# Two of each stage's weight rests computed by GpSimd instead of VectorE, in a fused 12-stage fp32 block kernel

## What is computed

```python
def swiglu(x, w13, w2):
    a, b = jnp.split(x @ w13, 2, axis=-1)
    return (jax.nn.silu(a) * b) @ w2
for l in range(DEPTH):        # first block
    x = layer_norm(ALPHA * x + 0.5 * swiglu(x, ffn1_w13[l], ffn1_w2[l]), ln_g[l, 0], ln_b[l, 0])
    m = mixer(x, w_in[l], ...)
    x = layer_norm(ALPHA * x + m, ln_g[l, 1], ln_b[l, 1])
    x = layer_norm(ALPHA * x + 0.5 * swiglu(x, ffn2_w13[l], ffn2_w2[l]), ln_g[l, 2], ln_b[l, 2])
for layer in range(DEPTH):    # second block
    h = swiglu_2(rms_norm(x, g[0]), ffn_w_in[layer, 0], ffn_w_out[layer, 0])
    x = x + 0.5 * rms_norm(h, g[1])
    h = token_mixer(rms_norm(x, g[2]), mix_w_in[layer], ...)
    x = x + rms_norm(h, g[3])
    h = swiglu_2(rms_norm(x, g[4]), ffn_w_in[layer, 1], ffn_w_out[layer, 1])
    x = x + 0.5 * rms_norm(h, g[5])
```

## Time and profile before

| what | value |
|---|---|
| median of 3 runs | 2111.23 us |
| the profiled execution, its own time | 2110.42 us |
| its span, first to last instruction | 2108.7 us |
| TensorE busy (matmuls) | 2092.6 us, 99% |
| VectorE busy | 1685.4 us, 80% |
| ScalarE busy | 1082.3 us, 51% |
| GpSimd busy | 80.7 us, 4% |
| granted TensorE clock | 1.000 |

### The profile page before, as it was taken

The page is one execution under the profiler, slowest core; times in us unless marked ns, Lnnn a source line. Parts: engine busy times, 40 slices in busy tenths (PEclk is TensorE's granted clock), DMA queues, the critical chain, the costliest instruction groups (busy, mean ns, idle before and its releaser), DMA issues.

```text
span 2108.7 us, 28912 instructions
## 1 busy us (share of the span) xinstructions
PE 2092.6 (99%) x10580; PEld 1776.2 (84%) x10580; DVE 1685.4 (80%) x3158; ACT 1082.3 (51%) x1568; POOL 80.7 (4%) x128
## 2 busy tenths in 40 slices
PE   9999999999999999999999999999999999999998
PEld 7888999888888899988878887988887888888887
DVE  6888766888888867778888887779888888678886
ACT  5445554544544455444454446575445445766443
POOL 0000010000000000000000001010000000101000
PEclk9999999999999999999999999999999999999999
DMA  7765755666566584557656766346665765645663
GB/s 249 235 194 175 221 168 156 188 218 191 177 218 193 176 234 143 187 168 224 196 153 213 215 190 196 126 135 208 212 197 166 225 192 168 185 140 161 211 191 106
DMA packets 314368, 395.56 MB, mean 188 GB/s; under 512 B 17972, under 2 KB 272212, under 8 KB 313972
## 3 DMA queue, kind: packets, MB, share of 16 engines
q1 hardware_dynamic: 309120, 375.52, 58.0%
q0 software_dynamic: 4944, 18.14, 2.7%
q10 hardware_dynamic: 164, 0.06, 0.0%
HBM read 392.59 MB, written 1.06 MB: 187 GB/s over the span
## 4 chain that ended last, share of the span: by engine, by line
PE 94%; DVE 3%; ACT 1%; issue 1%; DMA 0%; POOL 0%; DVEq 0%; POOLq 0%; SPq 0%; ACTq 0%
PE bank L310 26%; PE bank L312 26%; PE bank L311 26%; PE bank L304 4%; PE bank L305 4%; PE bank L306 4%; DVE w_lo L294 1%; PE bank L491 1%; PE bank L1472 1%; PE bank L1493 1%; PE bank L1002 1%; PE bank L1564 1%; ACT w_hi L287 0%; DVE xh L831 0%; DVE x L806 0%
## 5 line engine op out<-in xcount | busy, mean ns | idle before, releaser
L287 ACT ACTIVATE w_hi<-stage 128x1024 fp32r<-128x1024 f32 x711 | 746.8, 1058 | 635.4 <-PE bank L312 537.5
L294 DVE TENSOR_TENSOR w_lo<-stage,w_hi 128x1024 fp32r<-128x1024 f32 x711 | 864.8, 1224 | 213.6 <-ACT w_hi L287 206.6
L310 PE MATMUL bank<-w_hi,xt_hi 128*128 128x512 f32 x1760 | 692.0, 393 | 6.5 <-DVE xt_lo L846 5.6
L312 PE MATMUL bank<-w_hi,xt_lo 128*128 128x512 f32 x1760 | 685.5, 389 | 0.0
L311 PE MATMUL bank<-w_lo,xt_hi 128*128 128x512 f32 x1760 | 685.3, 389 | 0.0
L477 DVE STREAM_TRANSPOSE hidden<-hidden 32x128 f32<-32x128 f32 (+1 forms) x1376 | 391.7, 285 | 21.3
L310 PEld LDWEIGHTS bank<-w_hi,xt_hi 128*128 128x128 f32 x1760 | 330.5, 188 | 77.2 <-DVE xt_lo L846 4.6
L312 PEld LDWEIGHTS bank<-w_hi,xt_lo 128*128 128x128 f32 x1760 | 330.4, 188 | 69.1
L311 PEld LDWEIGHTS bank<-w_lo,xt_hi 128*128 128x128 f32 x1760 | 330.6, 188 | 66.4
L310 PE MATMUL bank<-w_hi,mt_hi 128*128 128x512 f32 x768 | 303.3, 395 | 0.2 <-DVE mt_lo L561 0.2
L312 PE MATMUL bank<-w_hi,mt_lo 128*128 128x512 f32 x768 | 299.4, 390 | 0.0
(11 more groups left out here) (279 smaller groups left out, 1387.5 us busy)
## 6 DMA issues: line engine op xcount, KB each, us to landing
stage<-in_ffn_w SPq DMA_DIRECT2D x352, 256.0 KB, 3.2
stage<-in_ffn_w_in SPq DMA_DIRECT2D x352, 256.0 KB, 3.2
stage<-in_ffn_w SPq DMA_DIRECT2D x88, 512.0 KB, 3.7
stage<-in_ffn_w_out SPq DMA_DIRECT2D x88, 512.0 KB, 3.7
stage<-in_w_in SPq DMA_DIRECT2D x80, 512.0 KB, 3.9
stage<-in_mix_w_in SPq DMA_DIRECT2D x56, 512.0 KB, 4.2
stage<-in_w_out SPq DMA_DIRECT2D x16, 512.0 KB, 4.2
stage<-in_mix_w_out SPq DMA_DIRECT2D x16, 512.0 KB, 3.5
```

The source lines that it names most:

```text
L287: act.activation(w_hi[:, u % RING, :], stage[:, u % STAGED, :], ACT.Copy).then_inc(S["hi_ready"], 1)
L294: dve.tensor_tensor(w_lo[:, u % RING, :], stage[:, u % STAGED, :], f32(w_hi[:, u % RING, :]), ALU.subtract).then_inc(S["lo_ready"], 1)
L310: pe.matmul(o, m_hi, hi, start=first, stop=False)
L312: return pe.matmul(o, m_lo, hi, start=False, stop=last)
```

## The change

GpSimd takes the rests of units +4 and +5 of every stage but the first (22 units, `BY_POOL`). It does both in one go, after the power for tile 0 of the stage before and in front of everything else it has for that transition. They have a semaphore of their own, `lo_by_pool`, and whoever waited for `lo_ready` (TensorE in `unit`, SyncE in `load`) waits through `rest_taken` for the one that counts this unit. VectorE's calls of `lo_upto` end one unit earlier where the fifth and sixth unit were due. To make room for a semaphore, the small table steps that counted `lb_step` now count on in `tables_out`; those instructions are the same.

```diff
+BY_POOL = [f + k for f in FIRST[1:-1] for k in (4, 5)]
...
+        def rest_taken(eng, u):
+
+            if u in BY_POOL:
+                eng.wait_ge(S["lo_by_pool"], BY_POOL.index(u) + 1)
+            else:
+                eng.wait_ge(S["lo_ready"], u + 1 - sum(p < u for p in BY_POOL))
+
         def load(sp, u, *halves):
 
             if u >= STAGED:
-                sp.wait_ge(S["lo_ready"], u - STAGED + 1)
+                rest_taken(sp, u - STAGED)
...
             for u in range(lo_next[0], min(end, FIRST[-1])):
-                dve.wait_ge(S["hi_ready"], u + 1)
-                dve.tensor_tensor(w_lo[:, u % RING, :], stage[:, u % STAGED, :], f32(w_hi[:, u % RING, :]),
-                                  ALU.subtract).then_inc(S["lo_ready"], 1)
+                if u not in BY_POOL:
+                    dve.wait_ge(S["hi_ready"], u + 1)
+                    dve.tensor_tensor(w_lo[:, u % RING, :], stage[:, u % STAGED, :], f32(w_hi[:, u % RING, :]),
+                                      ALU.subtract).then_inc(S["lo_ready"], 1)
                 lo_next[0] = u + 1
 
+        def pool_rests(pool, s):
+
+            for u in (FIRST[s] + 4, FIRST[s] + 5):
+                pool.wait_ge(S["hi_ready"], u + 1)
+                pool.tensor_tensor(w_lo[:, u % RING, :], stage[:, u % STAGED, :], f32(w_hi[:, u % RING, :]),
+                                   ALU.subtract).then_inc(S["lo_by_pool"], 1)
+
         def unit(pe, u):
-            pe.wait_ge(S["lo_ready"], u + 1)
+            rest_taken(pe, u)
...
                 dve_norm_start(dve, s - 1, 1)
-                if STAGES[s - 1] == "mix2":
-                    dve_norm_var(dve, s - 1, 1)
+                if STAGES[s - 1] != "mix2":
+                    lo_upto(dve, b + (5 if STAGES[s - 1] == "ffn" else 6))
+                dve_norm_var(dve, s - 1, 1)
                 lo_upto(dve, b + 6)
-                if STAGES[s - 1] != "mix2":
-                    dve_norm_var(dve, s - 1, 1)
                 dve_norm_x(dve, s - 1, 1)
...
-                lo_upto(dve, b + n + 5)
+                lo_upto(dve, b + n + 4)
                 dve_xt(dve, s + 1, 0)
...
                 for t in range(NT):
                     pool_norm(pool, s, t)
+                    if t == 0 and s + 1 < len(STAGES):
+                        pool_rests(pool, s + 1)
                     if BLOCK2 <= s + 1 < len(STAGES):
                         pool_pre(pool, s + 1, t)
```

More of the change, by code:

```diff
@@ L112, in build @@
         S = {n: ctx.enter_context(nc.semaphore(n)) for n in PER}
-        for n in ("hi_ready", "lo_ready", "used", "x_in0", "x_in1", "x_rest", "first_half", "const_in", "rest_in", "ones_set", "tables_in",
-                  "tables_turned", "tables_out", "lb_step", "x_out", "held", "rows_in",
+        for n in ("hi_ready", "lo_ready", "lo_by_pool", "used", "x_in0", "x_in1", "x_rest", "first_half", "const_in", "rest_in", "ones_set", "tables_in",
+                  "tables_turned", "tables_out", "x_out", "held", "rows_in",
                   "gu_done0", "silu0", "silu1", "gated0", "gated1", "h_turned", "h_blocks",
@@ L875, in act_lower_bounds @@
         def act_lower_bounds(act):
-            act.wait_ge(S["lb_step"], 3)
-            act.activation(lb_tmp[:, 3:5, :], lb_tmp[:, 1:3, :], ACT.Exp).then_inc(S["lb_step"], 1)
+            act.wait_ge(S["tables_out"], 6)
+            act.activation(lb_tmp[:, 3:5, :], lb_tmp[:, 1:3, :], ACT.Exp).then_inc(S["tables_out"], 1)
         def dve_tables(dve):
@@ L887, in dve_tables @@
             mx = lb_tmp[:, 0, :]
-            dve.tensor_tensor(mx, lbr_tab[:, 0, :], lbr_tab[:, 1, :], ALU.max).then_inc(S["lb_step"], 1)
-            dve.wait_ge(S["lb_step"], 1)
+            dve.tensor_tensor(mx, lbr_tab[:, 0, :], lbr_tab[:, 1, :], ALU.max).then_inc(S["tables_out"], 1)
+            dve.wait_ge(S["tables_out"], 4)
             for l in range(2):
-                dve.tensor_tensor(lb_tmp[:, 1 + l, :], lbr_tab[:, l, :], mx, ALU.subtract).then_inc(S["lb_step"], 1)
+                dve.tensor_tensor(lb_tmp[:, 1 + l, :], lbr_tab[:, l, :], mx, ALU.subtract).then_inc(S["tables_out"], 1)
         def dve_lower_bounds(dve):
             mx, e = lb_tmp[:, 0, :], lb_tmp[:, 3:5, :]
[L895 to L904, removed]
+            dve.wait_ge(S["tables_out"], 7)
+            dve.tensor_tensor(lb_tmp[:, 5, :], e[:, 0, :], e[:, 1, :], ALU.add).then_inc(S["tables_out"], 1)
+            dve.wait_ge(S["tables_out"], 8)
+            dve.reciprocal(mx, lb_tmp[:, 5, :]).then_inc(S["tables_out"], 1)
+            dve.wait_ge(S["tables_out"], 9)
+            dve.tensor_tensor(lb_tab[:, 1, :], e[:, 1, :], mx, ALU.mult).then_inc(S["tables_out"], 1)
+            dve.memset(lb_tab[:, 0, :], 0.0).then_inc(S["tables_out"], 1)
+            dve.wait_ge(S["tables_out"], 11)
+            dve.tensor_scalar(om_tab, lb_tab, -1.0, 1.0, ALU.mult, ALU.add).then_inc(S["tables_out"], 1)
+            dve.wait_ge(S["tables_out"], 12)
         def w_cols(w, c0, n, k0=0, nk=KD):
@@ L1166, in dve_mix1 @@
             dve_norm_start(dve, s - 1, 1)
+            lo_upto(dve, base + 5)
+            dve_norm_var(dve, s - 1, 1)
             lo_upto(dve, base + 6)
-            dve_norm_var(dve, s - 1, 1)
             dve_norm_x(dve, s - 1, 1)
```

## The result

| kernel | median | lowest to highest | runs |
|---|---|---|---|
| before | 2111.15 us | 2110.16 to 2111.27 | 4 |
| with the change | 2138.07 us | 2137.54 to 2138.86 | 4 |

The ratio is 1.0127, 95% interval [1.0115, 1.0139]: slower by 26.9 us. The sign was forecast, and 2138 lies in the range (2112 to 2141), but the forecast of 2128 took in only 16.7 of the 26.9 us, and 2138 is above the 2120 to 2137 that the prediction gave its own mechanism.

What follows compares the result with a forecast made beforehand. TensorE (PE) bounds the kernel, busy 2092.6 of 2108.7 us; a possible 6.9 us gain is lost to holds. Losses 2.3 + 10.2 + 4.2 = 16.7 us on 2110.4, with the median 0.8 higher, give 2128 us; range 2112 to 2141.

Steps and rivals of the forecast that it cites:

- Whether it runs beside VectorE: GpSimd's reads and VectorE instructions with two SBUF inputs exclude each other; waiting GpSimd goes first; PSUM readers are free.
- How long a rest takes: GpSimd's subtraction of 1024 columns, estimated from its selections: 2.0 us, lower end 1.04, upper end 3.1.
- D: Duration of one rest on GpSimd, taken as 2.0 us.
- R: Time in which a rest on GpSimd reads, taken as 1.9 us.
- Into stages 1, 3, 4: GpSimd's first rest goes before VectorE's of +3; `xt_lo` later by R - 1.13 = 0.8 us each, 2.3 in all.
- Into stages 6, 7, 9, 10: Both GpSimd rests hold VectorE; `xt_lo` later by 2R - 1.13 = 2.7 us each, 10.2 in all, less stage 6's 0.5.
- Into stages 8 and 11: Tile 1's power queues behind GpSimd's rest of +5; x late by D + 0.1 = 2.1 us each, 4.2 in all.
- Into stages 2 and 5, and SyncE's queue: The hold on VectorE is covered by its wait for `xt_hi`; loads queued behind rests have cover enough: 0 us.
- One hold instead of two: Rival: GpSimd's second rest waits out VectorE's rest of +3; stages 6, 7, 9, 10 lose 0.8 us each; 2120, chance 0.11.
- Hardly held: Rival: VectorE runs between pieces of GpSimd's reads; 6.9 us gain less 4.2 of stages 8 and 11; 2108.5, chance 0.10.
- faster: Rival: VectorE hardly held and both tensors read at once, D = 1.04; 4.6 us won, 2106.6, chance 0.10.
- Far slower: Rival: GpSimd's rest takes 3 us and more, or VectorE's PSUM reads are held too; 2141 and above, chance 0.09.

Runs made afterwards that it cites:

- early_fourth: Against the kernel before: GpSimd takes only unit +4's rest in stages 1, 3, 4, 6, 7, 9, 10, without waiting for VectorE's rest of +3; 2122.89 us.
- halves_6_7_9_10: Against the kernel before: GpSimd takes the two rests of stages 6, 7, 9, 10 only, each as two instructions of 512 columns; 2115.83 us.
- norm_first_8_11: Against the kernel before: GpSimd's rests in stages 8 and 11 only, +4 after tile 0's power and +5 after tile 1's; 2113.84 us.
- only_1_3_4: Against the kernel before: GpSimd takes the two rests of stages 1, 3 and 4 alone; 2114.51 us, ratio 1.0015.
- only_2_5: Against the kernel before: GpSimd takes the two rests of stages 2 and 5 alone; 2112.43 us, ratio 1.0006.
- late_fourth: Against the kernel before: GpSimd takes only +4's rest in stages 1, 3, 4, 6, 7, 9, 10, after VectorE's rest of +3; 2106.09 us.
- warm: The changed kernel with 12 transposes of a constant before the wait for x into stages 6, 7, 9, 10, 8 and 11; 2136.72 us.
- only_8_11: Against the kernel before: GpSimd takes the two rests of stages 8 and 11 alone; 2119.50 us, ratio 1.0037.

## Why the prediction was right, and where it was short

- **PE bounds, and only its waits at the transitions count.** The place was right: every loss stands at the eleven transitions. That PE's waits are all of it was not, as below.
- **Whether it runs beside VectorE (it does not).** Right, by two rows of short instructions: the earlier trace rows showed in small what `early_fourth`, `halves_6_7_9_10` and `norm_first_8_11` show in full. The Trainium skill (SBUF - State Buffer, Who interferes with whom) says that a VectorE instruction with at most one SBUF input, outside the modes with two ports, does not contend with GpSimd; the trace agrees: all 48 of `xt_lo` after the change take 0.67 to 0.69 us, and the 10 into stages 1 to 5 lie under a rest of GpSimd.
- **How long a rest takes.** D was 2.40 us for 2.0, R 2.2 for 1.9. The pace of the selections over one tensor was the wrong row to lean on for an operation over two. The figure of the Trainium skill (GPSIMD Engine Reference, 3.1 Elementwise; 2.25 us as an estimate from it) was nearer, and still 6% low. In the sum this is 3 x 0.3 for stages 1, 3, 4, up to 4 x 0.6 for 6, 7, 9, 10 and 2 x 0.4 for 8 and 11: with D and R as measured the prediction's own formulas give 3 x 1.1 + (4 x 3.3 - 0.5) + 2 x 2.5 = 21.0, which is 2132.
- **Into stages 1, 3, 4.** 2.3 forecast, 3.5 measured as gaps (3.1 by `only_1_3_4`); the formula with R = 2.2 gives 3.2, so it was the size of R.
- **Into stages 6, 7, 9, 10.** The mechanism was right, both holds are in the timeline, and 10.2 stand against 10.9 us of gaps. But the term is short by the 7.1 us of slower matmuls in the same transitions, and this is the largest error. Part of it replaces gaps: with R = 2.2 the formula gives 12.7, against 18.0 for both together. What the prediction would look for in the trace was also misplaced: it named waits for `xt_lo` of about 3.5 us in these four. The waits are 2.1 us for x in front of the second transposes (into stage 6, 2.8 in front of the first and 1.6 in front of the second), and at most 1.4 for `xt_lo`.
- **Into stages 8 and 11.** 4.2 forecast, 4.7 of gaps and 1.2 of pace. `norm_first_8_11` shows that GpSimd's order was the cause: with the power in front, the gaps of 2.4 us fall to 1.0. That the rest of +5 would hold x if it came in its turn was not considered.
- **Into stages 2 and 5, and SyncE's queue: nothing.** Nearly right for 2 and 5: 0.3 us each, in `only_2_5` as in the whole kernel. The prediction looked only at `xt_lo`, which is covered, and not at PE's second transposes, which wait for the held x. PE shows no new wait for a unit.
- **The step that failed** is the one that was not there: the sum took PE's pace as given. The earlier trace rows and the granted clock of 1.000 describe a kernel whose PE never stood for over 0.9 us at a transition. Most of the change's waits of 2 us and more came with stretches at half clock, which cost 1.0 to 2.3 us of pace a transition, 8.3 in all. The formulas with D and R as measured give 21.0 us, and the eleven transitions lost 28.0: some 7 us are left for the clock.
- **The range.** It held 2138 by luck. Its upper end, 2141, was set for a rest that lasts 3.1 us; the rest lasted 2.40, and what filled the room was the slower matmuls, which no term or rival had.
- **The rivals.** *One hold instead of two* fell with the 3.40 us of the rest of +3 into stage 7. *Hardly held* and *faster* fell with the holds. *Far slower* fell with D = 2.40 and the undisturbed PSUM readers. The gain of 6.9 us that the forecast saw behind the holds was real: `late_fourth` has 5.5 of it.

## What to carry to other kernels

In these traces, work given to GpSimd ran free beside VectorE instructions that read PSUM, and never beside one with two SBUF inputs: one of the two engines waited each time. Put it where VectorE reads PSUM, if need be by a wait that makes GpSimd come later, and keep it off the chain that TensorE waits for; if it must come in a busy stretch, instructions of half the length halved the hold here. A wait of TensorE of about 2 us and more may be charged a second time, by the slower matmuls behind it: in this kernel that was 0 to 1.6 us for each stretch of 3.4 us, on top of the wait.

## What was not expected of the hardware

- The two engines take strict turns at the border of instructions. With GpSimd's rest cut in two halves, each hold of VectorE fell from 2.2 us to 1.1, and the second half did not follow the first without a turn of VectorE between.
- After waits of 2.1 to 2.8 us (in `warm` also of 1.9 to 2.0), or from within them, the granted clock of TensorE was 0.50 for 3.4 or 6.8 us, and the matmuls of 512 columns followed each other at 0.43 us for 0.23. The same wait came with it in one execution and not in another: into stage 8 in `only_8_11` and not in the changed kernel, into stage 6 in the changed kernel and not in `warm`. Twelve transposes of 1.47 us in the wait did not keep the clock up into 7, 9 and 10. What decides this is open.
